# Attention heads taken in pairs, with projections cut into half units and a new merge order, in a two-layer hybrid trunk

## The chip, the cores and the metric

One Trainium2 chip, one core of it. The metric is the device time of the whole program in microseconds, median of the runs, lower is better. Two kernels of this case are told apart when they differ by over 0.2%.

## What is computed

Two layers, each of a half-step SwiGLU FFN, a token-mixing block and a second FFN, on x of 512 tokens by 1024 channels in float32. The mixing block reads one normalised input through one projection (`w_in`) and sums three gated branches:

```python
h = rms_norm(x, mix_norm[i])
z = h @ w_in[i]
y_a = dilated_attention_mixture(q, k, v)      # 3 groups x 4 heads of 64
y_b = spatial_gating(u, v, ...)               # chunked gMLP
y_c = multiscale_pool(z[..., C_OFF:G_OFF], ...)
gates = jax.nn.sigmoid(z[..., G_OFF:] + b_gate[i])
merged = (gates[0] * (y_a @ w_proj_a[i]) + gates[1] * (y_b @ w_proj_b[i])
          + gates[2] * (y_c @ w_proj_c[i]))
x = x + merged @ w_out[i]
```

In the attention, head slot j of the three groups is one softmax over all the keys of the three windows. The sequence is split into 4 residues r (tokens t with t mod 4 = r), so there are 4 x 4 = 16 (head, residue) items in a layer, `ATT = 16`, each with 128 queries and 768 keys (512 of group 0, 128 of each of the others).

## The kernel before, in words

**Large products.** A weight unit is 1024 x 256 float32, loaded to `raw[slot]` by SP's queue (`load`), then split in two parts: ScalarE (ACT) copies it rounded to `w_hi[slot]` (L737), VectorE (DVE) makes `w_lo = raw - w_hi` (L1030). TensorE (PE) does three products (hi*hi, lo*hi, hi*lo) for each of 2 column halves c and 8 k-tiles: 48 matmuls of 128x128 by 128x512 to a unit, into `psum[0]` or `psum[1]`. There are two slots, so a unit is split while the one ahead of it is multiplied: ACT's `split` waits for `unit_done` of the unit two back, PE's `unit()` waits for `split_made`, SP's `load` waits for `split_made` of the unit two back.

**The attention phase.** After the value projection and the three query/key units of heads 0 and 1, the remaining 6 units (3 query/key units of heads 2 and 3, 3 gate units of the first merge column) are interleaved with the 16 items. The order is written out by hand: 18 slots of 16 projection matmuls (L444, `part`), `attended(s)` says which item a slot holds. In a slot PE does: `scores` of the next item (L619: 3 float32 matmuls that read 64 rows of `qk`, 2 passes each, so 6 instructions, into `side[0]`), 8 projection matmuls, `transposes` of this item's probabilities (L629, 6 into `side[1]`), 8 projection matmuls, `values` (L641, 6 float32 matmuls in 12 instructions that write 64 rows of `side[1]`). DVE adds the mask and takes the maximum (L1340), negates it (L1344), later the reciprocal (L1349) and the scaling (L1350, `p_made`). ACT takes the exponential (L941), copies the transposed tile to `pT` (L963) and the head's output to `ya_hi` (L926); DVE makes `ya_lo` (L1329, `head_made`). Heads j even lie on rows 0 to 63 of `qk` and `side[1]`, j odd on rows 64 to 127. The order of items is head by head, four residues each, so that neighbours mostly share their rows. Projection outputs alternate between `psum[0]` and `psum[1]` by unit and DVE takes a whole unit (`take_unit`: L1309 twice, or L1052).

**The merge.** For each of 4 column pairs: gate units g = 0, 1, 2 from h (48 matmuls each), then `project`: `ya` (12 matmuls, w_proj_a), `yb` (24, w_proj_b), `yc` (24, w_proj_c). DVE multiplies the gates with them (L1392, L1395, L1401), ACT does the sigmoids (L934). Then 4 output units, banks in the order `OUT_BANKS`.

Of the kernel before, what the change touches and what calls it, by code (L numbers as in the profile page):

```python
# [18 lines left out]
F32 = mybir.dt.float32  # L19
# [56 lines left out]
def trunk(nc, x, ffn1_norm, ffn1_w_gate, ffn1_w_up, ffn1_w_down, mix_norm, w_in, b_gate, b_ln_g,  # L76
# [16 lines left out]
    ATT = HEADS * RES  # L93
    KEYS = S + 2 * P
# [5 lines left out]
    EV0, EV1 = 47, 47  # L100
# [4 lines left out]
    with ExitStack() as ctx:  # L105
# [48 lines left out]
        pT = at("pT", M + 42 * KB_, KEYS)  # L154
# [52 lines left out]
        unit_done = sem("unit_done")  # L207
        evacuated = [sem(f"evacuated{s}") for s in range(2)]
# [43 lines left out]
        SLOTS = 18  # L252
# [7 lines left out]
        OUT_BANKS = (2, 1, 0, 1)  # L260

        def attended(s):

            if s in (0, 9) or not 0 < s < SLOTS:
                return None
            return s - 1 if s < 9 else s - 2
# [6 lines left out]
        def _(sp):  # L273
# [40 lines left out]
            with rounds(sp, DEPTH, counts, split_made=UNITS_PER_LAYER) as layer:  # L314
# [83 lines left out]
        def _(pe):  # L398
# [39 lines left out]
            def part(dst, w, x_hi, x_lo, q0, q1):  # L438

                whi, wlo = w  # L440
                for q in range(q0, q1):
                    c, k, n = q // (3 * KD), q // 3 % KD, q % 3
                    l, r = ((whi, x_hi), (whi, x_lo), (wlo, x_hi))[n]
                    mm = nc.tensor.matmul(dst[:, c * S:(c + 1) * S], l[:, k * UNIT_N + c * P:k * UNIT_N + (c + 1) * P],  # L444
                                          r[:, k * S:(k + 1) * S], start=(k == 0 and n == 0), stop=(k == KD - 1 and n == 2))
                return mm

# [70 lines left out]
            with rounds(pe, DEPTH, counts, unit=UNITS_PER_LAYER, ev0=EV0, ev1=EV1,  # L518
                        sv0=8 + ATT, sv1=4, h=3 * D_PAIRS, acc=3 * (1 + KD), act=2 * FF_UNITS, w_sT=1, pooled=4,
                        vb=1, p=ATT, pT=ATT, head=ATT, y=2, merged=D_PAIRS) as layer:  # L520
# [88 lines left out]
                def scores(n):  # L609
                    j, r = divmod(n, RES)  # L610
                    rows_ = slice((j % 2) * HEAD_DIM, (j % 2 + 1) * HEAD_DIM)
                    t = qk[j // 2]
                    o = begin_side(0)
                    col = 0
                    for g in range(GROUPS):
                        q, k = g * S + r * P, (GROUPS + g) * S
                        keys = t[rows_, k:k + S] if g == 0 else t[rows_, k + r * P:k + (r + 1) * P]
                        width = S if g == 0 else P
                        mm = nc.tensor.matmul(o[:, col:col + width], t[rows_, q:q + P], keys, start=True, stop=True)  # L619
                        col += width  # L620
                    mm.then_inc(side_done[0], 1)

                def transposes(n):

                    pe.wait_ge(p_made, counts["p"].next())

                    pe.wait_ge(head_made, counts["head"].next())
                    for c in range(KEYS // P):
                        mm = nc.tensor.transpose(side[1][:, c * P:(c + 1) * P], p_tile[n % 2][:, c * P:(c + 1) * P], ident[:, :])  # L629
                    mm.then_inc(pT_written, 1)  # L630

                def values(n):
                    j, r = divmod(n, RES)

                    pe.wait_ge(pT_made, counts["pT"].next())
                    out_rows = slice((j % 2) * HEAD_DIM, (j % 2 + 1) * HEAD_DIM)
                    o = side[1][out_rows, KEYS:KEYS + P]
                    for c in range(KEYS // P):
                        g, t = (0, c) if c < TILES else (c - TILES + 1, r)
                        col = t * A_WIDTH + g * A_OUT + j * HEAD_DIM  # L640
                        mm = nc.tensor.matmul(o, v[:, col:col + HEAD_DIM], pT[:, c * P:(c + 1) * P],  # L641
                                              start=(c == 0), stop=(c == KEYS // P - 1))
                    mm.then_inc(head_done, 1)

                pair_of = (0, 1, 0, 1, 0, 1)
                STEP = 3 * 2 * KD // 6
                for s in range(SLOTS):
                    m, third = divmod(s, 3)
                    this, after = attended(s), attended(s + 1)
                    if third == 0:  # L650
                        o = begin(pair_of[m])
                        w = unit()
                    if this is not None and after is not None:
                        scores(after)

                    start, end = 2 * STEP * third, 2 * STEP * (third + 1)
                    before, between = (STEP, STEP) if s < SLOTS - 1 else (STEP // 2, STEP - 2)
                    part(o, w, h_hi, h_lo, start, start + before)
                    if this is None:
                        if s == 0:  # L660

                            pe.wait_ge(side_evacuated[1], counts["sv1"].now(1))

                        pe.wait_ge(evacuated[1 - pair_of[m]], counts[f"ev{1 - pair_of[m]}"].now(1))
                        scores(after)
                    else:
                        transposes(this)
                    mm = part(o, w, h_hi, h_lo, start + before, start + before + between)
                    if third == 2 and s < SLOTS - 1:
                        mm.then_inc(unit_done, 1)  # L670
                    if this is not None:
                        values(this)
                part(o, w, h_hi, h_lo, start + before + between, end).then_inc(unit_done, 1)

                def project():
# [3 lines left out]
                pe.wait_ge(head_made, counts["head"].now(1))  # L681
                pe.wait_ge(y_ready, counts["y"].next(2))
                project()
                with rounds(pe, D_PAIRS - 1, counts, unit=6, ev0=3, ev1=3):
                    for s in (1, 0, 1):
                        columns(begin(s), unit(), h_hi, h_lo, range(KD), True, True).then_inc(unit_done, 1)
                    project()
# [36 lines left out]
        def _(act):  # L724
# [105 lines left out]
            with rounds(act, DEPTH, counts, unit=UNITS_PER_LAYER, raw0=8 * UNITS_PER_LAYER + 16 * 2,  # L830
                        raw1=8 * UNITS_PER_LAYER + 16 * 3, ev0=EV0, ev1=EV1, se0=8 + ATT, act=2 * FF_UNITS,
                        sd0=7 + ATT, sd1=4, ln=1, yb=2, neg=ATT, pT_written=ATT, head=ATT, merged=D_PAIRS) as layer:
# [84 lines left out]
                counts["sd0"].next(ATT)  # L917
# [3 lines left out]
                def head_hi(n):  # L921
                    j, r = divmod(n, RES)
                    rows_ = slice((j % 2) * HEAD_DIM, (j % 2 + 1) * HEAD_DIM)
                    act.wait_ge(head_done, counts["head"].next())
                    dst = ya_hi[rows_, (j // 2) * S:(j // 2 + 1) * S].rearrange("p (i r) -> p r i", r=RES)[:, r, :]
                    nc.scalar.activation(dst, side[1][rows_, KEYS:KEYS + P],  # L926
                                         ACT.Copy).then_inc(ya_hi_made, 1)
# [10 lines left out]
                def exponential(n):  # L938

                    act.wait_ge(neg_max_made, counts["neg"].next())  # L940
                    nc.scalar.activation(p_tile[n % 2][:, :], p_tile[n % 2][:, :], ACT.Exp, bias=neg_max[:, n % 2:n % 2 + 1],  # L941
                                         accum_out=row_sum[:, n % 2:n % 2 + 1]).then_inc(exp_made, 1)

                bias_col = T_BGATE + layer * (3 * KD)
                next_unit = [dict(parts=2), dict(parts=2), {}, {}, {}, dict(k=KA)]
                for s in range(SLOTS):
                    m, third = divmod(s, 3)
                    if attended(s - 1) is not None:
                        head_hi(attended(s - 1))
                    if third == 0:  # L950
                        if m > 0:
                            counts["unit"].next()
                            if m - 1 < 3:
                                counts[f"ev{(m - 1) % 2}"].next()
                        split(**next_unit[m])
                    if third == 1 and m > 3:
                        sigmoids(m - 4, (m - 1) % 2, bias_col)
                    if third == 1 and m > 3:

                        exponential(attended(s + 1))  # L960
                    if attended(s) is not None:
                        act.wait_ge(pT_written, counts["pT_written"].next())
# [495 lines left out]
```

## Time and profile before

| | |
|---|---|
| median of 3 runs | 2417.64 us (2417.22 to 2418.68) |
| the profiled execution's own time | 2416.66 us |
| its span, first to last instruction | 2414.9 us |
| mean granted TensorE clock | 0.997 |
| busy: PE, PE's weight loads, DVE, ACT, POOL | 99%, 82%, 45%, 30%, 1% |
| chain that ended last | PE 97%, ACT 1%, DVE 1% |
| two attention phases | 129.66 us each, 288 of the large matmuls and 16 items in each |

The span is between the first and the last instruction of the profiled execution; what lies around it is 1.76 us. A matmul's record lasts longer than its turn on the engine, since matmuls are pipelined: what a matmul takes in a stream is the distance from its start to the next one's start. An item is a (head, residue) pair as above.

### The profile page before, as it was taken

How to read it: one execution, taken by the hardware profiler on the slowest of the kernel's cores; microseconds unless marked ns; L12 is line 12 of the kernel's file. 1: busy time of each engine (PE TensorE's matmuls, PEld its weight loads, DVE VectorE, ACT ScalarE, POOL GpSimd, SP SyncE). 2: the span in 40 equal slices, each digit the busy share in tenths (PEclk: the TensorE clock that was granted, in tenths of full speed). 3: DMA queues.
4: the chain of work that ended last, by engine and by line, in shares of the span. 5: the costliest groups of instructions: out<-in, count | busy, mean ns of one | idle time of the engine just before them, and what ended most of it. 6: DMA issues, size and time to landing. Idle time of an engine off the chain costs nothing.

```text
span 2414.9 us, 27466 instructions
## 1 busy us (share of the span) xinstructions
PE 2394.2 (99%) x11021; PEld 1969.6 (82%) x11021; DVE 1095.0 (45%) x1045; ACT 716.6 (30%) x665; POOL 30.5 (1%) x58
## 2 busy tenths in 40 slices
PE   7999999999999999999999999999999999999999
PEld 6888888887788888888888888888777888888887
DVE  7444435544454554443344443365544445544433
ACT  4222223323422332222232222232334223322222
POOL 4000000000000000000000000000000000000000
PEclk9999999999999999999999999999999999999999
DMA  4333223321132323322332332332312233232221
GB/s 141 94 97 104 81 98 122 95 81 40 40 104 87 114 89 102 104 89 95 96 101 91 104 100 84 96 116 79 88 31 66 83 109 109 91 104 91 96 96 65
DMA packets 229756, 221.81 MB, mean 92 GB/s; under 512 B 4161, under 2 KB 227505, under 8 KB 229681
## 3 DMA queue, kind: packets, MB, share of 16 engines
q1 hardware_dynamic: 225696, 215.29, 28.4%
q10 hardware_dynamic: 3984, 5.51, 0.7%
q8 instruction: 48, 0.79, 0.1%
q14 instruction: 28, 0.22, 0.0%
HBM read 218.69 MB, written 2.10 MB: 91 GB/s over the span
## 4 chain that ended last, share of the span: by engine, by line
PE 97%; ACT 1%; DVE 1%; issue 0%; DMA 0%; ACTq 0%; DVEq 0%
PE psum L433 83%; PE psum L444 5%; PE side L641 2%; PE psum L561 2%; PE side L619 2%; PE side L433 1%; PE psum L453 1%; PE side L629 1%; DVE acc L1087 0%; PE side L571 0%; PE side L543 0%; DMA x_in<-in_x_dram 0%; ACT gate L934 0%; PE side L582 0%; ACT L941 0%
## 5 line engine op out<-in xcount | busy, mean ns | idle before, releaser
L433 PE MATMUL psum<-h_hi,w_hi 128*128 128x512 f32 x1984 | 776.0, 391 | 8.7 <-DVE w_lo L1030 8.5
L433 PE MATMUL psum<-h_lo,w_hi 128*128 128x512 f32 x1984 | 772.8, 390 | 0.0
L433 PE MATMUL psum<-h_hi,w_lo 128*128 128x512 f32 x1984 | 772.7, 389 | 0.0
L1030 DVE TENSOR_TENSOR w_lo<-raw,w_hi 128x2048 fp32r<-128x2048 f32 (+2 forms) x224 | 470.9, 2102 | 338.5 <-ACT w_hi L737 337.8
L737 ACT ACTIVATE w_hi<-raw 128x2048 fp32r<-128x2048 f32 (+2 forms) x224 | 393.8, 1758 | 601.9 <-PE psum L433 578.1
L433 PEld LDWEIGHTS psum<-h_hi,w_hi 128*128 128x128 f32 x1984 | 373.0, 188 | 88.5 <-issue 9.2
L433 PEld LDWEIGHTS psum<-h_hi,w_lo 128*128 128x128 f32 x1984 | 373.0, 188 | 77.9
L433 PEld LDWEIGHTS psum<-h_lo,w_hi 128*128 128x128 f32 x1984 | 373.1, 188 | 77.7 <-issue 1.2
L433 PE MATMUL psum<-act_hi,w_hi 128*128 128x512 f32 x704 | 273.9, 389 | 0.0
L433 PE MATMUL psum<-act_lo,w_hi 128*128 128x512 f32 x704 | 273.9, 389 | 0.0
L433 PE MATMUL psum<-act_hi,w_lo 128*128 128x512 f32 x704 | 273.9, 389 | 0.0
L793 ACT ACTIVATE act_hi<-us 128x1024 f32 (+1 forms) x44 | 46.7, 1061 | 455.0 <-DVE us L1118 455.0
L1052 DVE TENSOR_TENSOR us<-psum,rstd 128x1024 f32<-128x1024 f32 x44 | 53.9, 1225 | 276.5 <-PE psum L433 276.5
L433 PEld LDWEIGHTS psum<-act_hi,w_lo 128*128 128x128 f32 x704 | 132.2, 188 | 27.5
L433 PEld LDWEIGHTS psum<-act_lo,w_hi 128*128 128x128 f32 x704 | 132.2, 188 | 27.5
L433 PEld LDWEIGHTS psum<-act_hi,w_hi 128*128 128x128 f32 x704 | 132.2, 188 | 27.2
L1052 DVE TENSOR_TENSOR gs<-psum,rstd 128x1024 f32<-128x1024 f32 x44 | 53.9, 1225 | 119.4 <-PE psum L433 118.9
L1120 DVE TENSOR_TENSOR act_lo<-us,act_hi 128x1024 f32 (+1 forms) x44 | 53.9, 1226 | 58.7 <-ACT act_hi L793 58.7
L755 ACT ACTIVATE us<-xT 128x1024 f32<-128x1024 f32 x24 | 25.4, 1059 | 185.1 <-DVE xT L1065 185.1
L444 PE MATMUL psum<-h_hi,w_hi 128*128 128x512 f32 x192 | 77.8, 405 | 0.0
L444 PE MATMUL psum<-h_hi,w_lo 128*128 128x512 f32 x192 | 77.7, 405 | 0.0
L444 PE MATMUL psum<-h_lo,w_hi 128*128 128x512 f32 x192 | 77.4, 403 | 0.0
(185 smaller groups left out, 1942.4 us busy)
## 6 DMA issues: line engine op xcount, KB each, us to landing
raw<-in_ffn_w_gate_dram SPq DMA_DIRECT2D x44, 1024.0 KB, 5.3
raw<-in_ffn_w_up_dram SPq DMA_DIRECT2D x44, 1024.0 KB, 5.3
raw<-in_w_in_dram SPq DMA_DIRECT2D x42, 1024.0 KB, 5.3
raw<-in_ffn_w_down_dram SPq DMA_DIRECT2D x32, 1024.0 KB, 4.9
raw<-in_ffn_w_down_dram SPq DMA_DIRECT2D x16, 768.0 KB, 4.2
raw<-in_w_in_dram SPq DMA_DIRECT2D x24, 512.0 KB, 4.4
raw<-in_w_out_dram SPq DMA_DIRECT2D x8, 1024.0 KB, 5.0
raw<-in_w_proj_b_dram SPq DMA_DIRECT2D x8, 512.0 KB, 3.4
```

Source lines behind the costliest of these rows:

```text
L433: mm = nc.tensor.matmul(dst[:, c * S:(c + 1) * S], l[:, a], r[:, b], start=first and k == ks[0] and n == 0, stop=last and k == ks[-1] and ...
L444: mm = nc.tensor.matmul(dst[:, c * S:(c + 1) * S], l[:, k * UNIT_N + c * P:k * UNIT_N + (c + 1) * P], r[:, k * S:(k + 1) * S], start=(k == ...
L453: mm = nc.tensor.matmul(o, l[:, k * P:(k + 1) * P], r[:, k * S:(k + 1) * S], start=(k == 0 and n == 0), stop=(k == KD - 1 and n == 2))
L561: mm = nc.tensor.matmul(d, l[:, k * S + t * P:k * S + (t + 1) * P], r[:, b], start=(k == 0 and m == 0), stop=(k == KD - 1 and m == 2))
L619: mm = nc.tensor.matmul(o[:, col:col + width], t[rows_, q:q + P], keys, start=True, stop=True)
L641: mm = nc.tensor.matmul(o, v[:, col:col + HEAD_DIM], pT[:, c * P:(c + 1) * P], start=(c == 0), stop=(c == KEYS // P - 1))
L737: nc.scalar.activation(w_hi[s][:, 0:k * n], raw[s][:, 0:k * n], ACT.Copy).then_inc(hi_made, 1)
L755: nc.scalar.activation(sq[:, :], pair(xT, d), ACT.Square).then_inc(sq_made, 1)
L793: nc.scalar.activation(pair(act_hi, i), us[:, :], ACT.Copy).then_inc(act_hi_made, 1)
L1030: nc.vector.tensor_tensor(w_lo[s][:, a], raw[s][:, a], w_hi[s][:, a].bitcast(F32), ALU.subtract).then_inc(split_made, 1)
L1052: return nc.vector.tensor_tensor(dst, two(psum[s][:, :]), rstd2, ALU.mult)
L1120: nc.vector.tensor_tensor(pair(act_lo, i), us[:, :], pair(act_hi, i).bitcast(F32), ALU.subtract).then_inc(act_ready, 1)
```

## The change

Items are taken as 8 pairs, `PAIRS = 8`: pair n holds residue r = n mod 4 of heads 2*jp and 2*jp+1, jp = n div 4. PE does both items' scores one after the other (the first into `side[0]`, the second into `psum[1]`), then both items' values of the pair ahead of it (`pT[0]`, `pT[1]`), then projection matmuls, then both items' transposes (into `side[1]`, then `side[0]`), then projection matmuls. All matmuls of the first head stand ahead of the second's. The 288 projection matmuls of the phase are one stream cut at positions `SCORES_AT` and `TURNS_AT`; their outputs go to the two halves of `psum[0]` alone, and DVE takes them by half unit (24 matmuls), told by `half_done` or `unit_done`. `ya_hi` and `ya_lo` are made once for a pair, on 128 rows. On ACT the copy of a pair's outputs (`head_hi`) and, for some pairs, the split of a unit stand ahead of the two exponentials. The merge order is yb, ya, yc with the banks swapped, and PE waits for the last head only ahead of the first ya. No arithmetic is added or taken away.

```diff
+    PAIRS = ATT // 2
-        pT = at("pT", M + 42 * KB_, KEYS)
+        pT = [at("pT0", M + 42 * KB_, KEYS), at("pT1", M + 85 * KB_, KEYS)]
+        half_done = sem("half_done")
+        scored_b = sem("scored_b")
-        SLOTS = 18
+        PHASE = 6 * 2 * 3 * KD
+        SCORES_AT = (10, 48, 86, 124, 162, 194, 226, 258)
+        TURNS_AT = (38, 76, 114, 152, 185, 217, 249, 281)
-        OUT_BANKS = (2, 1, 0, 1)
+        OUT_BANKS = (0, 2, 0, 1)
-                    for w in (w_proj_a, w_proj_b, w_proj_c):
+                    for w in (w_proj_b, w_proj_a, w_proj_c):
...
+                def project_to(end):
+                    for q in range(stream["at"], end):
+                        h, k, n = q // (3 * KD), q // 3 % KD, q % 3
+                        c = h % 2
+                        if q % (3 * KD) == 0:
+                            pe.wait_ge(evacuated[0], free + max(h - 1, 0))
+                            if c == 0:
+                                stream["w"] = unit()
...
+                        if k == KD - 1 and n == 2:
+                            mm.then_inc(half_done if c == 0 else unit_done, 1)
+                def score_pair(n):
+                    jp, r = divmod(n, RES)
+                    t = qk[jp]
+                    outs = (begin_side(0), begin(1))
+                    if n == RES:
+                        pe.wait_ge(evacuated[0], free + 6)
+                    for b in range(2):
+                        for g in range(GROUPS):
...
+                            mm = nc.tensor.matmul(outs[b][:, col:col + k1 - k0], t[rows_of(b), q:q + P], t[rows_of(b), k0:k1],
+                                                  start=True, stop=True)
+                            if g == GROUPS - 1:
+                                mm.then_inc((side_done[0], scored_b)[b], 1)
+                def turn_pair(n):
+                    pe.wait_ge(p_made, counts["p"].next())
...
+                    for c in range(KEYS // P):
+                        mm = nc.tensor.transpose(side[1][:, c * P:(c + 1) * P], p_tile[0][:, c * P:(c + 1) * P], ident[:, :])
+                    mm.then_inc(pT_written, 1)
+                    pe.wait_ge(p_made, counts["p"].next())
+                    o = begin_side(0)
...
+                def value_pair(n):
+                    pe.wait_ge(pT_made, counts["pT"].next())
+                    pe.wait_ge(side_evacuated[0], counts["sv0"].now(1 if n == PAIRS - 1 else 0))
                     pe.wait_ge(head_made, counts["head"].next())
+                    for b in range(2):
+                        for c in range(KEYS // P):
...
+                            mm = nc.tensor.matmul(side[1][rows_of(b), KEYS:KEYS + P], v[:, col:col + HEAD_DIM],
+                                                  pT[b][:, c * P:(c + 1) * P], start=(c == 0), stop=(c == KEYS // P - 1))
+                for n in range(PAIRS):
+                    project_to(SCORES_AT[n])
+                    score_pair(n)
+                    if n > 0:
+                        value_pair(n - 1)
+                    project_to(TURNS_AT[n])
+                    turn_pair(n)
+                project_to(PHASE)
+                value_pair(PAIRS - 1)
+                def project(last_head=False):
+                    columns(begin(1), unit(), yb_hi, yb_lo, range(KB), True, True).then_inc(unit_done, 1)
+                    if last_head:
+                        pe.wait_ge(head_made, counts["head"].now(1))
                     columns(begin(0), unit(), ya_hi, ya_lo, range(KA), True, True).then_inc(unit_done, 1)
-                    columns(begin(1), unit(), yb_hi, yb_lo, range(KB), True, True).then_inc(unit_done, 1)
-                    columns(begin(0), unit(), yc_hi, yc_lo, range(KB), True, True).then_inc(unit_done, 1)
+                    columns(begin(1), unit(), yc_hi, yc_lo, range(KB), True, True).then_inc(unit_done, 1)
...
+                for n in range(PAIRS):
+                    if n == 0:
+                        step(parts=2)
+                    if n > 0:
+                        head_hi(n - 1)
+                    if n == 1:
+                        step(parts=2)
+                    if n == 5:
+                        step()
+                    for b in range(2):
+                        exponential(b)
+                    if n in (2, 3):
+                        step()
+                    if n == 6:
+                        step(KB)
+                    take_turned()
+                    if n in (5, 6):
+                        counts["ev0"].next()
+                        sigmoids(n - 5, 0, bias_col)
+                head_hi(PAIRS - 1)
...
+                for n in range(PAIRS):
+                    score_max(n)
+                    if n > 0:
+                        head_lo(n - 1)
+                    normalise(0)
+                    normalise(1)
+                    if n < 4:
+                        take_half((0, 2, 3, 5)[n])
+                        split()
+                        if n in (0, 2):
+                            take_half((1, None, 4)[n])
+                    elif n in (4, 7):
+                        take_half(6 if n == 4 else 10)
+                        take_half(7 if n == 4 else 11)
+                    elif n == 5:
+                        split()
+                        take_half(8)
+                    else:
+                        take_half(9)
+                        split(KB)
+                head_lo(PAIRS - 1)
```

In this diff the second of the three blocks on ACT and the third on DVE (`for n in range(PAIRS)`) are each engine's own order. `take_turned` is ACT's copy of both transposed tiles (L963 twice), `score_max` DVE's masked maximum and negation for both items, `step` a split (ACT's L737).

## Rows read from the trace of the kernel before

**Rows 1.** The page: busy time of the engines, and the chain by engine.

```profile
PE 2394.2 (99%) x11021; PEld 1969.6 (82%) x11021; DVE 1095.0 (45%) x1045; ACT 716.6 (30%) x665; POOL 30.5 (1%) x58
PE 97%; ACT 1%; DVE 1%; issue 0%; DMA 0%; ACTq 0%; DVEq 0%
```

**Rows 2.** Both attention phases by windows: length, busy us (instructions), clock.

```profile
525.42:655.08 129.66, 128.27 (x674) 96.98 (x672) 57.04 (x127) 53.11 (x79) 0.00 (x0) 1.00 0.14 43
1715.17:1844.83 129.66, 128.26 (x673) 96.95 (x672) 57.04 (x127) 53.11 (x79) 0.00 (x0) 1.00 0.14 43
```

**Rows 3.** The chain in time order, first phase: start, length, what.

```profile
525.59 1.81 PE psum L444 x8
...
538.42 1.50 PE side L619 x6
539.92 2.04 PE psum L444 x8
541.96 0.66 PE side L629 x6
542.61 1.84 PE psum L444 x8
544.45 1.46 PE side L641 x12
```

**Rows 4.** Timeline of PE around group changes: start, length of the records.

```profile
544.06 0.39 PE L444 MATMUL psum<-h_hi,w_lo 128*128 128x512 f32 x1
544.38 0.32 PE L641 MATMUL side<-pT,v 128*64 128x128 f32 x1
...
545.63 0.27 PE L641 MATMUL side<-pT,v 128*64 128x128 f32 x1
545.84 0.69 PE L619 MATMUL side<-qk 64*128 64x512 f32 x1
546.37 0.81 PE L619 MATMUL side<-qk 64*128 64x512 f32 x3
...
547.13 0.27 PE L619 MATMUL side<-qk 64*128 64x128 f32 x1
547.33 0.50 PE L444 MATMUL psum<-h_hi,w_hi 128*128 128x512 f32 x1
547.67 0.40 PE L444 MATMUL psum<-h_lo,w_hi 128*128 128x512 f32 x1
```

**Rows 5.** Timeline of PE, three places where it waited for another engine.

```profile
592.36 0.69 PE L619 MATMUL side<-qk 64*128 64x512 f32 x1 [0.95 <-DVE qk L1309]
...
624.61 1.28 PEld L641 LDWEIGHTS side<-pT,v 128*64 128x64 f32 x12 [0.56 <-ACT pT L963]
...
647.45 0.19 PEld L641 LDWEIGHTS side<-pT,v 128*64 128x64 f32 x2 [0.73 <-ACT pT L963]
...
544.38 0.19 PEld L641 LDWEIGHTS side<-pT,v 128*64 128x64 f32 x2 [0.36 <-issue]
```

**Rows 6.** DVE and ACT by groups, 520 to 660 us: busy, mean ns.

```profile
L1340 DVE CUSTOM_DVE_ANT_0 p_tile<-side,masks 128x768 f32<-128x768 f32 x16 | 15.3, 954 | 9.6 <-issue 9.6
L1350 DVE TENSOR_SCALAR p_tile<-p_tile,small 128x768 f32<-128x768 f32 x16 | 9.9, 620 | 0.6
L941 ACT ACTIVATE p_tile<-p_tile,small 128x768 f32<-128x768 f32 x16 | 14.9, 931 | 4.7 <-DVE small L1344 4.7
L963 ACT ACTIVATE pT<-side 128x768 f32<-128x768 f32 x16 | 13.0, 811 | 43.8 <-PE side L629 43.8
L941 ACT ACT_TABLE_LOAD x3 | 3.8, 1283 | 0.1
```

**Rows 7.** Timeline of DVE and ACT, one split, one merge step.

```profile
546.13 1.92 ACT L737 ACTIVATE w_hi<-raw 128x2048 fp32r<-128x2048 f32 x1
...
655.28 1.23 DVE L1052 TENSOR_TENSOR gate<-psum,rstd 128x1024 f32<-128x1024 f32 x1 [0.78 <-PE psum L444]
656.42 1.22 DVE L1030 TENSOR_TENSOR w_lo<-raw,w_hi 128x1024 fp32r<-128x1024 f32 x1
```

More of the change, by code:

```diff
@@ L436, in columns @@
                 return mm
[L438 to L446, printed above, removed]
             def one_column(o, w):
@@ L623, in transposes @@
-                def transposes(n):
-                    pe.wait_ge(p_made, counts["p"].next())
-                    pe.wait_ge(head_made, counts["head"].next())
[L628 to L672, printed above, removed]
@@ L673, in _, with rows_of @@
-                part(o, w, h_hi, h_lo, start + before + between, end).then_inc(unit_done, 1)
-                def project():
+                def rows_of(b):
+                    return slice(b * HEAD_DIM, (b + 1) * HEAD_DIM)
+                free = counts["ev0"].next()
+                counts["ev0"].next(PHASE // (3 * KD) - 1)
+                stream = dict(at=0, w=None)
+                def project_to(end):
[6 more added lines that the diff above has]
+                                stream["w"] = unit()
+                        whi, wlo = stream["w"]
+                        l, r = ((whi, h_hi), (whi, h_lo), (wlo, h_hi))[n]
+                        mm = nc.tensor.matmul(psum[0][:, c * S:(c + 1) * S], l[:, k * UNIT_N + c * P:k * UNIT_N + (c + 1) * P],
+                                              r[:, k * S:(k + 1) * S], start=(k == 0 and n == 0), stop=(k == KD - 1 and n == 2))
+                        if k == KD - 1 and n == 2:
+                            mm.then_inc(half_done if c == 0 else unit_done, 1)
+                    stream["at"] = end
@@ L921, in head_hi @@
                 def head_hi(n):
[L922 to L927, printed above, removed]
+                    jp, r = divmod(n, RES)
+                    act.wait_ge(head_done, counts["head"].next(2))
+                    dst = ya_hi[:, jp * S:(jp + 1) * S].rearrange("p (i r) -> p r i", r=RES)[:, r, :]
+                    nc.scalar.activation(dst, side[1][:, KEYS:KEYS + P], ACT.Copy).then_inc(ya_hi_made, 1)
                 def sigmoids(g, s, col):
@@ L946, in _ @@
[L946 to L962, printed above, removed]
-                        nc.scalar.activation(pT[:, :], side[1][:, 0:KEYS], ACT.Copy).then_inc(pT_made, 1)
-                    if attended(s + 1) is not None and not (third == 1 and m > 3):
-                        exponential(attended(s + 1))
@@ L966, in _, with take_turned @@
-                head_hi(ATT - 1)
-                counts["unit"].next()
+                    nc.scalar.activation(p_tile[b][:, :], p_tile[b][:, :], ACT.Exp, bias=neg_max[:, b:b + 1],
+                                         accum_out=row_sum[:, b:b + 1]).then_inc(exp_made, 1)
+                def take_turned():
+                    act.wait_ge(pT_written, counts["pT_written"].next())
+                    nc.scalar.activation(pT[0][:, :], side[1][:, 0:KEYS], ACT.Copy).then_inc(pT_made, 1)
+                    act.wait_ge(pT_written, counts["pT_written"].next())
+                    nc.scalar.activation(pT[1][:, :], side[0][:, 0:KEYS], ACT.Copy).then_inc(side_evacuated[0], 1)
@@ L969, in project @@
+                head_hi(PAIRS - 1)
+                counts["ev0"].next()
                 def project(d, col):
-                    step(KB)
-                    sigmoids(2, 1, col)
+                    step(KA)
+                    sigmoids(2, 0, col)
                     step(KB)
                     step()
-                    counts["ev0"].next(2)
-                    counts["ev1"].next()
+                    counts["ev1"].next(2)
+                    counts["ev0"].next()
                     act.wait_ge(merged_made, counts["merged"].next())
@@ L984, in _ @@
                     for g in range(3):
-                        step(KA if g == 2 else UNIT_K)
+                        step(KB if g == 2 else UNIT_K)
                         if g < 2:
-                            sigmoids(g, 1 - g % 2, col)
+                            sigmoids(g, g % 2, col)
                     project(i + 1, col)
@@ L1010, in _ @@
                                            "silu", "act_hi", "gelu", "ln_std", "yc_hi", "yb_hi", "exp",
-                                           "head", "gate", "merged", "pooled", "y")}
+                                           "head", "gate", "merged", "pooled", "y", "half", "scored_b")}
             counts |= {k: Count(1) for k in ("ev0", "ev1", "se0", "se1")}
@@ L1348, in normalise @@
+                    dve.wait_ge(evacuated[1], v_)
+                    negate(1)
+                def normalise(b):
                     dve.wait_ge(exp_made, counts["exp"].next())
-                    chain(nc.vector.reciprocal(row_inv[:, b], row_sum[:, b]))
-                    nc.vector.tensor_scalar(p_tile[n % 2][:, :], p_tile[n % 2][:, :], row_inv[:, b], None,
+                    chain(nc.vector.reciprocal(row_inv[:, b:b + 1], row_sum[:, b:b + 1]))
+                    nc.vector.tensor_scalar(p_tile[b][:, :], p_tile[b][:, :], row_inv[:, b:b + 1], None,
@@ L1368, in _ @@
-                for s in range(SLOTS):
-                    m, third = divmod(s, 3)
-                    if attended(s - 1) is not None:
-                        head_lo(attended(s - 1))
-                    if third == 0 and m > 0 and attended(s) is None:
-                        take_unit(m - 1)
-                    if attended(s + 1) is not None:
-                        score_max(attended(s + 1))
-                    if third == 0:
-                        split(UNIT_K if m < 5 else KA)
-                        if m > 0 and attended(s) is not None:
-                            take_unit(m - 1)
-                    if attended(s + 1) is not None:
-                        normalise(attended(s + 1))
@@ L1387, in project @@
+                head_lo(PAIRS - 1)
                 def project(d):
+                    step(KA)
+                    dve.wait_ge(gate_made, counts["gate"].next(2))
+                    evac(1, nc.vector.tensor_tensor(gate[1][:, :], gate[1][:, :], psum[1][:, :], ALU.mult))
                     step(KB)
-                    dve.wait_ge(gate_made, counts["gate"].next())
-                    evac(0, nc.vector.tensor_tensor(gate[0][:, :], gate[0][:, :], psum[0][:, :], ALU.mult))
-                    step(KB)
```

117 lines of the change are left out of this document (58 added, 59 removed).

## The prediction, made blind

> **What bounds the kernel now.** I read the page first: PE is busy 99% of the span and is 97% of the chain that ended last, while DVE and ACT are at 45% and 30% [rows 1]. The reader is to see that time can only come out of PE's own stream. Then the windows on the two attention phases: 129.66 us each, clock 1.00 (that is 2.4 GHz), PE never truly idle [rows 2]. Busy shares can't say more, so I went to the chain in order of time and to the timeline of PE, where starts can be subtracted.
>
> The large matmuls follow each other at 1.81 / 8 = 0.227 us [rows 3]. One ordinary item takes 1.50 + 2.04 + 0.66 + 1.84 + 1.46 = 7.50 us [rows 3]. What would its instructions take if they merely followed each other? 16 large matmuls: 3.63. Scores: two passes of 512 columns and four of 128. Records two to four of them begin 0.54 apart, the last three 0.11 apart, so 2 x 0.43 + 4 x 0.11 = 1.30 [rows 4]. Transposes 0.65, near their row. Values 12 x 0.109 = 1.31 (544.38 to 545.63 is 1.25 for 11 steps, the first being longer) [rows 4]. Sum 6.89. So 0.61 us of each item is paid for changing between kinds of matmul. The starts show where [rows 4]: large matmul to values 0.32 in place of 0.23 (0.09) and a long first step (0.05); values to scores 0.21 in place of 0.11 (0.10); first to second score 0.53 in place of 0.43 (0.10); scores to large 0.20 in place of 0.11 (0.09); first to second large 0.34 in place of 0.23 (0.11). That is 0.54, and some 0.06 is spread over the large matmuls behind a change. The transposes cost nothing of the kind: they use the whole array, as the large ones do.
>
> For the phase: 288 x 0.2267 + 16 x 3.26 = 65.3 + 52.1 = 117.4, so 129.66 - 117.4 = 12.2 us are overhead. Of these about 1.5 are true waits: 0.95 for DVE's `qk` ahead of the scores of the ninth item, and two waits for ACT's `pT` beyond the ordinary 0.36: 0.56 - 0.36 = 0.20 and 0.73 - 0.36 = 0.37 [rows 5]. The other 10.7 are the changes, 0.67 an item.
>
> **Fewer changes of kind.** In a pair, large -> scores A, B -> values A, B -> large -> transposes A, B -> large: the chain of changes that one item paid is paid once for two. Eight pairs pay 8 x 0.54 = 4.3 us. The spread part of 0.06 an item I keep at 1.0. Overhead after: 5.3 in place of 10.7, a gain of 5.4 us a layer.
>
> **The waits that go.** The ninth item's scores no longer stand right behind the last query/key unit: half 5 ends at position 144, DVE takes it in pair 3, and pair 4's scores stand at 162, 18 matmuls or 4 us on. The two `pT` waits came of sigmoids and two table loads (1.28 us each [rows 6]) ahead of the copy on ACT; now the sigmoids stand behind the copy. Gain 1.5 us a layer, if no wait takes their place (next part).
>
> **The switch of head inside a pair** has no row: no two neighbours in the trace use different 64-row halves for scores or different output halves for values. There are 2 such switches in each of 16 pairs. Below: the second head's first instruction starts together with the first head's last, and saves one 0.11 step: 32 x 0.11 = -3.5 us. Above: each costs what a change of kind costs around scores (0.10 + 0.10): 32 x 0.20 = +6.4 us. The nearest row is the passage between large matmuls and transposes, same kind of use of the array and no cost; I take 0.
>
> The Trainium skill, TensorEngine Tiling (Array Packing), Key Properties, says that changing the tiling mode drains the engine and that changing only the tile does not, and that different tiles run in parallel. The 0.2 us steps of rows 4 agree with the first half. By its second half the sum would go to the low bound, 3.5 us lower; by the row of same-kind passages it is 0.
>
> **Does a new wait arise?** From a pair's first score S, by the rows: A's scores end at S + 1.6, B's at S + 2.9; DVE's maxima (0.95 and small steps) end at 2.8 and 4.1. Values of the pair before run from 2.8 to 5.6. ACT is held behind them: `head_hi` 5.7 to 6.1, then exponentials (0.93 and 0.1 for the sum) to 7.1 and 8.1 [rows 6]. DVE scales (reciprocal, then 0.62) by 8.0 and 9.0. PE reaches the transposes after 28 large matmuls, at 5.66 + 28 x 0.227 = 12.0 (23 in pairs 4 to 7: 10.9), B's at 11.6. Slack 1.9 us or more. Pairs 1 and 5 have a split (1.92 [rows 7]) ahead of the exponentials: scaled at 9.9 and 10.9 against 10.9 and 11.6 in pair 5, slack 0.6. Pair 6 has a table load, 1.28: slack 1.2. Behind the transposes ACT copies both tiles (2 x 0.81): the second ends 1.2 us after them, the next scores come 9 or 10 matmuls later, 2.1 us, and the last values 7 matmuls later, 1.7 us, slack 0.45. ACT's split in pair 3 waits for the unit that ends at position 144, 10.6, and ends at 12.5, when PE is only at the first transpose. DVE: in pairs 0 and 2 it waits in `take_half` until a half unit is over, some 15.1 at the latest, and ends at 16.1; the next pair's first maximum is due at 15.7 + 1.6 = 17.3 (pair 0: 14.2 against 14.5). The halves' banks are free one pair ahead. DMAs: every load still waits on the split two units back, 10 us or more before its own split. Price of all that: 0; if the cover in pair 5 were gone, 1 us for each 1 us of lateness, twice.
>
> **The half-size work.** `head_hi` and `head_lo` do 128 rows in one instruction, 16 fewer of each; neither is on the path: 0. Half-unit takes cost DVE the same operations, gates in two halves a little more, against 57 us of work in 129.66 [rows 2]: 0.
>
> **The merge order.** Before, `yb` (w_lo 1.22 us) is split while `ya`'s 12 matmuls (2.72 us) run, behind a take of 1.14: 656.42 + 1.22 = 657.64 against yb's start at 655.08 + 2.75 [rows 7]. After, it is `yc` that is split under `ya`, behind the product with gate 1, same lengths: slack again 0.15. Nothing gained or lost. At entry yb (5.4 us) covers the last head's copies, where six large matmuls did: 0 in both. If the slack failed: 0.2 us at 8 places, 1.6 us.
>
> **Sum.** 2 x (5.4 + 1.5) = 13.8 us. Against the profiled execution: span 2414.9 - 13.8 = 2401.1, with 1.76 around it 2402.9. The median shown stands 0.98 above that execution, so 2403.8.
>
> **The rivals.** (a) *Tiles overlap at the switch of head*: 2403.8 - 3.5 = 2400.3. For it the separate array halves, against it no row. Chance 0.25. (b) *The switch of head costs like a change of kind*: 2403.8 + 6.4 = 2410.2. For it that every other change among float32 groups cost 0.2; against it the free passage to the transposes. Chance 0.10. (c) *The gain is eaten by waits in some pairs*: pair 5 or 6 late by 1 to 2 us in both layers, some 2407. Chance 0.07. (d) *Slower*: PE stands at each pair's first transpose, because the path scores, maximum, values of the pair before, copy, exponential, scaling now holds two heads and ACT's `head_hi` stands ahead of both exponentials. It decides from 0.9 us a pair (13.8 / 16), which needs the path 1.9 + 0.9 = 2.8 us longer than its rows: 2420 if it is 3.2. Only the split's pairs come near. Chance 0.03. (e) *The phase is bound otherwise than by changes*, so that pairing moves nothing but the 3 us of waits: 2414.6; the starts in rows 4 speak against it. Chance 0.02. The forecast itself: 0.53.
>
> **Numbers.** The range goes from 2399.5 (a, with 0.8 for the sum's rounding) to 2408.5, leaving out most of (b), (d), (e) and a tail: 0.84 inside. The measurement tells 0.2%, 4.8 us; faster by more than that is all but (d), (e) and a little of (c): 0.94; within 0.03; slower 0.03.
>
> **What the profile after would show.** Attention phases of 122.7 us in place of 129.66; a pair of 15.7 us (14.4 in pairs 4 to 7); one 0.2 us step each at scores -> values and values -> large, none inside a pair (rival a: the second head's first record starts within some ns of the first's last; rival b: 0.2 to 0.3 apart). Waits of PE on `p_tile` or `pT` above 0.5 us would be (c) or (d). The merges should keep their lengths. The prediction is wrong if the phase is above 125 or below 120 us, or if time moves anywhere else.

## The result and the profile after

The changed kernel takes 2394.68 us (median of 4 runs, 2393.36 to 2395.02) against 2418.16 us for the kernel before in the same comparison: ratio 0.9902, 95% interval 0.9885 to 0.9919. It is 23.5 us faster. The forecast was 2403.8 us with a range down to 2399.5; the direction was right, the gain was 1.7 times the one forecast. Times of one kernel vary: its runs lie up to 1.7 us apart here, so the small effects below rest on lengths in the traces.

The first attention phase by windows, in the kernel after (columns as in [rows 2]); the second, 1703.99 to 1821.18, is as long:

```profile
525.86:643.05 117.19, 117.19 (x673) 92.94 (x671) 56.80 (x122) 48.87 (x70) 0.00 (x0) 1.00 0.16 48
```

Each phase has gone from 129.66 to 117.19 us, 12.47 us less, at the same clock. My sum said 122.7, and named a phase below 120 as a sign of being wrong. The phase even ended under the 117.4 us that I had worked out for a stream without any overhead, so instructions must run beside each other. The chain in order of time shows where, in one whole pair:

```profile
553.75 2.32 PE psum L616 x10
556.07 1.16 PE side L634 x3
557.23 0.11 PE psum L634
557.34 0.22 PE side L634 x2
557.57 0.97 PE psum L634 x5
558.54 2.38 PE side L663 x24
560.92 6.62 PE psum L616 x28
567.54 0.65 PE side L645 x6
568.19 0.66 PE side L650 x6
```

L616 are the large matmuls, L634 the scores (the first head's into `side`, the second's into `psum`), L663 the values, L645 and L650 the transposes. Read the four score lines: three of the first head's six instructions, then one of the second's, and only then the rest of the first's. A pair's scores take 1.16 + 0.11 + 0.22 + 0.97 = 2.46 us, where the terms of my sum come to 2.80 (1.50 for the first head, 1.30 for the second); 24 value instructions take 2.38, where they come to 2.77 (1.46 and 1.31). The timeline has the same seam by starts:

```profile
556.00 0.69 PE L634 MATMUL side<-qk 64*128 64x512 f32 x1
...
556.97 0.69 PE L634 MATMUL psum<-qk 64*128 64x512 f32 x1
557.07 0.49 PE L634 MATMUL side<-qk 64*128 64x128 f32 x3
```

The second head's first score (556.97) starts 0.1 us ahead of the last three of the first head, though it stands behind them in the program.

No wait took the place of the old ones: in the list of waits of this phase PE waits for no other engine, nor in that of the second phase, which answers to [rows 5]. The path over DVE and ACT was as worked out: in the tightest pair, pair 5, the scaled probabilities are ready 8.8 and 9.7 us after the first score, and PE comes for them at 10.2 and 10.9.

One thing got worse. In the merges, `yc` now starts late (DVE's timeline, then PE's weight loads, kernel after; these answer to [rows 7]):

```profile
695.32 1.22 DVE L1414 TENSOR_TENSOR gate<-gate,psum 128x1024 f32<-128x1024 f32 x1 [3.78 <-PE psum L432]
696.46 1.22 DVE L1037 TENSOR_TENSOR w_lo<-raw,w_hi 128x1024 fp32r<-128x1024 f32 x1
```

```profile
697.23 0.19 PEld L432 LDWEIGHTS psum<-ya_hi,w_lo 128*128 128x128 f32 x1
697.73 0.19 PEld L432 LDWEIGHTS psum<-yc_hi,w_hi 128*128 128x128 f32 x1 [0.32 <-DVE w_lo L1037]
```

`ya` starts at 694.96; DVE's product starts 0.36 us later, not 0.20 as a take did behind `ya` before, so `w_lo` is finished at 697.68, when PE already wants it. Together with a slower restart of PE that is some 0.2 us at three of the four merges of a layer, and 0.1 at the first, where the product starts 0.29 us behind `ya`. From the first `ya` or `yb` to the output units, layer 1 takes 153.18 us in place of 152.45, layer 2 153.13 in place of 152.43. Together 1.4 us lost.

The two traced executions differ by 21.6 us in span (2414.9 and 2393.3), less than the 24.9 us of the two phases minus 1.4. Of the 1.9 us between, 0.4 lie ahead of the first phase and 1.3 behind the last merges. There, in both kernels, the granted clock fell from 1.00 to 0.50 (1.2 GHz) while PE did its last transposes, 6.5 us ahead of the end in the kernel before and 9.9 us ahead of it in the kernel after, and the transposes then follow each other at 0.21 us in place of 0.11.

### The profile page after: what moved, and what is told of

It reads as the page before. It is cut to its first block, busy times and chain, and to the rows that moved or that the text cites. A ratio compares the mean times of both kernels' runs of the same rounds, so it can differ in the third digit from the quotient of the medians.

```text
span 2393.3 us, 27568 instructions
## 1 busy us (share of the span) xinstructions
PE 2374.8 (99%) x11021; PEld 1962.3 (82%) x11021; DVE 1091.7 (46%) x1035; ACT 707.8 (30%) x649; POOL 28.5 (1%) x58
## 4 chain that ended last, share of the span: by engine, by line
PE 98%; DVE 1%; DMA 0%; ACT 0%; issue 0%; ACTq 0%; DVEq 0%
PE psum L432 83%; PE psum L616 6%; PE psum L550 2%; PE side L663 2%; PE side L634 1%; PE side L432 1%; PE psum L442 1%; PE psum L634 1%; PE side L650 0%; PE side L645 0%; DMA x_in<-in_x_dram 0%; DVE acc L1094 0%; PE side L560 0%; PE side L532 0%; PE side L571 0%; DVE h_lo L1085 0%
## 5 line engine op out<-in xcount | busy, mean ns | idle before, releaser
L616 PE MATMUL psum<-h_hi,w_lo 128*128 128x512 f32 x192 | 76.4, 398 | 0.0
L616 PE MATMUL psum<-h_lo,w_hi 128*128 128x512 f32 x192 | 76.3, 397 | 0.0
L616 PE MATMUL psum<-h_hi,w_hi 128*128 128x512 f32 x192 | 76.2, 397 | 0.0
```

The lines of the kernel that those rows point to most:

```text
L616: mm = nc.tensor.matmul(psum[0][:, c * S:(c + 1) * S], l[:, k * UNIT_N + c * P:k * UNIT_N + (c + 1) * P], r[:, k * S:(k + 1) * S], start=( ...
```

## The experiments

All compare with the kernel before on the same chip (its medians there: 2417.34, 2416.95 and 2417.06 us in the three groups of four) and are told by their own median and phase length. The groups ran on different chips and the medians of the kernel before differ by up to 1.2 us between them and the first comparison, so a difference of that size between two groups tells nothing. "Theory" numbers start from 2394.7, the changed kernel's time. The edits are on the changed kernel, but for the one that says otherwise.

### Taking the overlap away at the scores

```diff
-  mm = nc.tensor.matmul(outs[b][:, col:col + k1 - k0], t[rows_of(b), q:q + P], t[rows_of(b), k0:k1],
+  mm = nc.tensor.matmul(outs[b][:, col:col + k1 - k0], t[rows_of(0), q:q + P], t[rows_of(0), k0:k1],
```

> Edit: in each pair the second head's score matmuls read the first head's 64 rows of qk (so both heads' scores are those of the first head), nothing else changes. Theory 1 (the 5.6 us a layer beyond my sum come from the second head's instructions running beside the last ones of the first, because they use other rows of the array): the overlap at the scores goes, the block of a pair's scores is 2.79 us as my sum had it in place of the 2.46 seen, phase 117.2 + 8 x 0.33 = 119.8 us, time 2394.7 + 5.3 = 2400. Theory 2 (the changes between kinds of matmul are cheaper in the new order, no overlap): nothing changes, 2394.7.

Measured: 2399.31 us, ratio 0.9924 (0.991 to 0.9937), phase 119.62 us. The chain of that kernel:

```profile
556.78 1.50 PE side L634 x6
558.28 1.30 PE psum L634 x6
559.58 2.38 PE side L663 x24
```

The first head's six now stand whole ahead of the second's six, 2.80 us together, as my sum had them. The values are untouched. What this kernel has and the changed one has not is one and the same set of rows for both heads, so the 2.4 us a phase are overlap of two row halves. The two heads still write different tiles (`side` and `psum`) in it, so those alone don't make the overlap.

### Taking it away at the values

```diff
-  mm = nc.tensor.matmul(side[1][rows_of(b), KEYS:KEYS + P], v[:, col:col + HEAD_DIM],
+  mm = nc.tensor.matmul(side[1][rows_of(0), KEYS:KEYS + P], v[:, col:col + HEAD_DIM],
```

> Edit: in each pair the second head's value matmuls write the first head's 64 output rows of the bank, so the second head's result takes the first's place and the other 64 rows keep what an earlier use left. Theory 1 (overlap of different array halves): the block of a pair's values is 2.76 us in place of 2.39, phase 117.2 + 8 x 0.37 = 120.2 us, time 2394.7 + 6 = 2400.7. Theory 2 (cheaper changes of kind): 2394.7.

Measured: 2399.11 us, 0.9926 (0.9912 to 0.9939), phase 120.03 us; the 24 value instructions take 2.76 us again:

```profile
558.78 2.76 PE side L663 x24
```

In this kernel the second head also writes the very addresses that the first wrote, so this run alone can't tell the shared half from the shared addresses. No run separates the two; at the scores the addresses stayed apart and the overlap went all the same.

### Both away: my own sum, measured

Both edits at once.

> Edit: both earlier edits together: the second head's scores read the first head's rows of qk and its values write the first head's output half (its result takes the first's place). All of the change stands but no two matmuls can use different halves of the array. Theory 1 (my sum for fewer changes of kind and vanished waits is right, 13.8 us, and the rest is overlap): phases of 119.6 + 120.0 - 117.2 = 122.4 us (my sum said 122.7), time 2394.7 + 10.5 = 2405. Theory 2 (the changes of kind are worth more than my sum and the two overlaps share a part): below 2401.

Measured: 2405.01 us, 0.9951 (0.9937 to 0.9964), phase 122.57 us, the sum having said 122.7. This is the kernel I had forecast: pairs, fewer changes of kind, no waits, no overlap. The chain, one pair:

```profile
557.07 1.50 PE side L634 x6
558.57 1.30 PE psum L634 x6
559.87 2.76 PE side L663 x24
```

The two single edits add (2.43 + 2.84 = 5.27 us of phase, 5.38 measured together). Two heads one after the other on the same half have no step between them, which is the 0 that my sum took; what it missed is what different halves give.

### One more change of kind

Four large matmuls moved between a pair's scores and the values of the pair before.

```diff
                     if n > 0:
+                        project_to(SCORES_AT[n] + 4)
                         value_pair(n - 1)
```

> Edit: four of the large projection matmuls move from behind a pair's values to between its scores and the values of the pair before (7 of 8 pairs); same matmuls, one more passage scores -> large -> values in place of scores -> values. Theory 1 (each change of kind costs what my starts gave: 0.09 and 0.11 and 0.09 more, 0.09 less, and 0.02 to 0.05 over the next ones): 0.22 x 7 x 2 = 3.1 us more, 2397.8, and up to 0.6 more if the later values make pair 5 wait. Theory 2 (changes of kind cost nothing, all of the gain was overlap and waits): 2394.7.

Measured: 2396.82 us, 0.9917 (0.9903 to 0.993), phase 118.63 us: 1.44 us more for 7 places, 0.21 us each (expected 0.22), 2.9 us in two layers. The time alone is 2.1 us more, which the noise between groups would not settle; the phase does. So one passage more has the price that the starts of [rows 4] gave it.

### The new merge order on the kernel before

```diff
-                    for w in (w_proj_a, w_proj_b, w_proj_c):
+                    for w in (w_proj_b, w_proj_a, w_proj_c):
...
-                    columns(begin(0), unit(), ya_hi, ya_lo, range(KA), True, True).then_inc(unit_done, 1)
-                    columns(begin(1), unit(), yb_hi, yb_lo, range(KB), True, True).then_inc(unit_done, 1)
+                    columns(begin(0), unit(), yb_hi, yb_lo, range(KB), True, True).then_inc(unit_done, 1)
+                    if last_head:
+                        pe.wait_ge(head_made, counts["head"].now(1))
+                    columns(begin(1), unit(), ya_hi, ya_lo, range(KA), True, True).then_inc(unit_done, 1)
...
-                    dve.wait_ge(gate_made, counts["gate"].next())
-                    evac(0, nc.vector.tensor_tensor(gate[0][:, :], gate[0][:, :], psum[0][:, :], ALU.mult))
+                    dve.wait_ge(gate_made, counts["gate"].next(2))
+                    evac(0, nc.vector.tensor_tensor(gate[1][:, :], gate[1][:, :], psum[0][:, :], ALU.mult))
```

> Edit: the kernel before with the new merge order alone (yb, ya, yc; loads, splits, gates and the wait for the last head moved with it). Theory 1 (the merge order is worth nothing): 2417.3. Theory 2 (ya first cost something at entry or in the splits): 1 to 2 us faster, 2416.

Measured: 2419.34 us over 11 runs against 2416.95, ratio 1.0009 (1.0000 to 1.0018): not faster, rather 2.4 us slower, at the edge of what the interval tells. Neither theory had this sign. The trace has the same late start as the changed kernel:

```profile
711.70 0.19 PEld L433 LDWEIGHTS psum<-yc_hi,w_hi 128*128 128x128 f32 x1 [0.32 <-DVE w_lo L1031]
```

The merges of the two layers are 0.65 and 0.59 us longer than in the kernel before, 1.2 us together. In this execution the first phase was also 1.58 us longer than the second, and that is the clock: from 594.9 to 598.3 us the granted clock was 0.50 (1.2 GHz), which happened inside a phase in no other trace of this case, and large matmuls follow each other there at 0.43 us in place of 0.23. PE had just waited 0.96 us for DVE's `qk`, but it waited as long in the kernel before, where the clock stayed at 1.00. So the 1.58 us are no part of the edit, and the other 1.2 us of the median's 2.4 stay open.

### The gate wait put ahead

```diff
-                    step(KA)
-
-                    dve.wait_ge(gate_made, counts["gate"].next(2))
+                    split(KA)
+                    dve.wait_ge(gate_made, counts["gate"].next(2))
+                    done()
```

> Edit: the changed kernel with DVE's wait for the two sigmoids ahead of its wait for yb's matmuls in the merge, so that one wait and not two lies between the end of yb and the product with gate 1. Theory 1 (in the new merge order that product starts 0.36 us after yb's successor ya and not 0.20 as before, so yc's w_lo is finished 0.05 us too late and PE's restart makes it 0.2 us a merge): 8 x 0.18 = 1.4 us less, merges of 5.44 us for yc, time 2393.3. Theory 2 (the slow start of yc has another cause): yc stays at 5.57, 2394.7.

Measured: 2393.02 us, 0.9898 (0.9883 to 0.9913). `yc` takes 5.44 to 5.49 us at every merge (before this edit 5.53 to 5.62). The same two operations, and PE's first load of `yc`:

```profile
695.18 1.22 DVE L1414 TENSOR_TENSOR gate<-gate,psum 128x1024 f32<-128x1024 f32 x1 [3.62 <-PE psum L432]
696.32 1.22 DVE L1037 TENSOR_TENSOR w_lo<-raw,w_hi 128x1024 fp32r<-128x1024 f32 x1
```

```profile
697.59 0.19 PEld L432 LDWEIGHTS psum<-yc_hi,w_hi 128*128 128x128 f32 x1 [0.15 <-DVE w_lo L1037]
```

`ya` starts at 694.98 here: the product now comes 0.20 us behind it and `yc`'s first load 0.14 us earlier than in the changed kernel. The wait for the sigmoids had nothing to wait for: ACT ended the last of them 2.5 us before `ya` started, in both kernels. The cause is shown by its places, and the merges of the two layers are 0.63 and 0.65 us shorter, 1.3 us together (expected 1.4); that the time is 1.7 us less agrees, but the two intervals overlap.

### Heads alternating, scores

```diff
-                    for b in range(2):
-                        for g in range(GROUPS):
+                    for g in range(GROUPS):
+                        for b in range(2):
```

> Edit: a pair's score matmuls alternate between the two heads (A1 B1 A2 B2 A3 B3) in place of A1 A2 A3 B1 B2 B3. Theory 1 (whatever stands within a few instructions and uses other rows runs beside it): two heads' scores take about one head's time, 1.30 + 0.1 + 0.2 = 1.6 us in place of 2.46 for a pair, 16 pairs, 2394.7 - 13.8 = 2381. Theory 2 (only the seam gains and every alternation costs as a change does, 0.1 to 0.2 us, 4 more of them in a pair): 2394.7 + 16 x 0.6 = 2404. Theory 3 (it makes no difference how they are ordered): 2394.7.

Measured: 2379.13 us, 0.984 (0.9826 to 0.9853), phase 109.50 us. Theory 1, with a little more than it promised (15.5 us in place of 13.8).

### Heads alternating, values

```diff
-                    for b in range(2):
-                        for c in range(KEYS // P):
+                    for c in range(KEYS // P):
+                        for b in range(2):
```

> Edit: a pair's value matmuls alternate between the two heads, 128 keys of each at a time. Theory 1 (overlap of different output halves): 1.31 + 0.05 + 0.2 = 1.56 us in place of 2.39 for a pair, 16 pairs: 2394.7 - 13.3 = 2381.4. Theory 2 (each alternation costs 0.1 or more, 10 more of them): 2394.7 + 16 = 2411. Theory 3 (only the depth of the overlap seen at the seam counts, no more): 2394.7.

Measured: 2379.23 us, 0.984 (0.9827 to 0.9854), phase 109.44 us; the 24 instructions take 1.46 us, those of a single item took 1.46 for 12 [rows 3].

### How far ahead PE looks: blocks of three and of two

```diff
-                    for b in range(2):
-                        for c in range(KEYS // P):
+                    for b, c in [(b, c) for c0 in range(0, KEYS // P, 3) for b in range(2) for c in range(c0, c0 + 3)]:
```

> Edit: the changed kernel with a pair's values in blocks of three matmuls (six instructions) of each head in turn, scores as changed. Theory 1 (an instruction can start once the one four places ahead of it has started, if the array half it needs is free: that is what the seam shows, where B's first starts with A's fourth from the last): two steps of 0.109 more than full alternation, 1.46 + 0.22 = 1.68 us a pair, 2379.2 + 3.5 = 2382.7. Theory 2 (each seam gains the 0.37 us seen, there are three now): 2.76 - 1.11 = 1.65, 2382.2, but with the first head's first block alone for four steps, not two.

Measured: 2384.5 us, 0.9862 (0.9847 to 0.9878), 1.73 us for the 24 (expected 1.68). The first record of the second head is at 558.247 beside the first head's third at 558.241, as theory 1 placed it; theory 2 had it two steps later. The block is 0.05 us longer than the two steps of theory 1, and the time 1.8 us above its 2382.7: by the phase, 111.96 us, a pair costs 0.32 us more than when alternating, where theory 1 had 0.22. So the rule gives the place, and not all of the price.

With 2 for 3 in the same line:

> Edit: the same in blocks of two matmuls (four instructions) of each head. Theory 1 (look ahead of four places): the second head's first instruction starts with the first head's first, as in full alternation: 1.46 us a pair, 2379.2. Theory 2 (0.37 us a seam, nothing to do with places; five seams, 1.85 us, but not below one head's time): also near 2379, so it is the start of the second head's first record, beside the first's first or not, that tells. Theory 3 (the look ahead is three places, not four): one step of 0.109 more in each block, 16 x 0.33 = 5 us more, 2384.

Measured: 2379.89 us, 0.9843 (0.983 to 0.9856), 1.51 us for the 24. The second head's first starts at 557.574, the first head's first at 557.560, so they start together: the fifth instruction starts with the first, and theory 3 (three places) is out. That it is no more than four places was told by the longer blocks: with five, the second head would have started beside the second instruction in blocks of six.

### Both alternating, then with the gate wait

> Edit: scores and values of a pair both alternate between the heads. Theory 1 (the two savings add): phases of 109.5 + 109.4 - 117.2 = 101.8 us, time 2394.7 - 30.9 = 2363.8. Theory 2 (a pair is now 1.9 us shorter, but the path of maximum, copy, exponential and scaling is not, so PE waits for p_tile in the pairs that have a split or a table load ahead of the exponentials, 0.5 to 1 us in each of up to 3 pairs a layer): 2365 to 2370.

Measured: 2363.02 us, 0.9777 (0.9763 to 0.979), phase 101.64 us (expected 101.8). No wait arose. Score starts of one pair, first head and second (their next instructions start at 553.62 and 553.63):

```profile
553.09 0.69 PE L634 MATMUL side<-qk 64*128 64x512 f32 x1
553.10 0.69 PE L634 MATMUL psum<-qk 64*128 64x512 f32 x1
```

> Edit: scores and values of a pair alternate between the heads, and DVE's wait for the sigmoids stands ahead of its wait for yb. Theory 1 (the two edits have nothing in common and add): 2363.0 - 1.4 = 2361.6, 0.977 of the kernel before. Theory 2 (a shorter phase leaves the first merge late, where the last pair's copies and splits come close): no gain from the second edit, 2363.0.

Measured: 2361.64 us, 0.9768 (0.9755 to 0.9781), `yc` at 5.44 to 5.46 us: 55 us faster than the kernel before, 33 us faster than the changed one, and the best version here.

## Why the prediction was wrong, point by point

**What bounds the kernel: right.** The two phases are 24.9 us shorter, and all of that is PE's stream.

**Fewer changes of kind, and waits gone: right in mechanism and size.** 5.4 + 1.5 = 6.9 us a layer were forecast. With the overlap taken away the phase is 122.57 us, 7.1 us less than 129.66: 14.2 us against 13.8. The price of one passage was measured again at 0.21 us by adding seven a layer. One part of the 5.4 had no row: the starts of [rows 4] give 8 x 0.54 = 4.3, the other 1.1 is what remained of the 10.7 us, and the 122.57 us say that it went too.

**The switch of head inside a pair: the step that failed.** I took 0 for it in the sum and, as the low bound, one step of 0.11 us for each of 32 switches, 3.5 us. A switch saves 0.30 us at the scores (119.62 - 117.19 over 8 pairs) and 0.36 at the values (120.03 - 117.19 over 8), 10.8 us in all when both are taken away together. Two things were wrong in my term. I let the nearest row, large matmuls followed by transposes, stand for a case it does not resemble: both of those use 128 rows and 128 columns, so that row says nothing of two different halves. And in the rival I let the second head start only together with the first head's last instruction, while it starts beside the fourth from last. The rule of the Trainium skill, TensorEngine Tiling (Array Packing), Key Properties, that different tiles load and multiply in parallel, is what the trace shows, with 24 value instructions in 1.46 us where one half alone needs 2.76. I had given it as a sentence beside the rival and a chance of 0.25; the runs say that it should have carried the forecast. Even so the rival's size was too small: its 2400.3 us is 5.6 us above the time measured.

**The bound that was too near.** A bound for something no row shows has to ask for the most that the mechanism could do, not for its smallest instance. Two heads beside each other all the way give 42 us against no overlap (2405.01 us with both heads on one half, 2363.02 with the heads alternating on two). The changed kernel keeps the heads in blocks and gets 10.8 of them; the forecast's range had no room for any of it beyond one step of 0.11 us a switch.

**No new wait: right.** The slack of the tightest pair was forecast at 1.0 and 0.7 us (10.9 against 9.9, 11.6 against 10.9, for which the prediction wrote 0.6), it is 1.4 and 1.2. That is not the overlap's doing, which moves both ends: in the kernel without overlap the probabilities are scaled at 9.5 and 10.5 and taken at 10.9 and 11.6, a slack of 1.4 and 1.1. My path was 0.4 us too long. In rival (d) one number is wrong: a path longer by 3.2 us gives 16 x 1.3 = 20.8 us and 2424.6 us, not 2420.

**The merge order: mis-sized.** I gave it 0 and a slack of 0.15 us, with 1.6 us as the price if the slack failed. It failed: DVE passes two waits between the end of `yb` and its product, and starts 0.36 us after `ya` in place of 0.20; by the rows the slack was 0.19 (657.83 against 657.64), and 0.16 of it went there. The price was near the one stated, 1.4 us.

Together: 14.2 us from pairing and the vanished waits, 10.8 us from overlap, 1.4 us lost in the merges, 23.6 against 23.5 measured. That they agree to 0.1 us is partly luck, since the runs of one kernel lie 1 to 2 us apart.

## What to carry to other kernels

Where two small matmuls use different halves of the array (other 64 rows for the operands, or other 64 output rows), let them alternate in the program: here the second one was nearly free (31.7 us on top of the change, 33 with the merge repair). Different output halves were tried only within one tile, `side`, and different operand rows only with outputs in two tiles. Blocks of one head at a time get only the few instructions at the seam. Grouping matmuls by kind is worth 0.2 us for each passage saved; and a wait that is already satisfied is not free (0.16 us here) when it stands in a path with a tenth of a microsecond of slack, so put it ahead of the one that is waited for.

## What the runs showed of the hardware that was not expected

Matmuls do not always start in program order. The second head's first score started at 556.97 us, ahead of three score instructions of the first head that stand before it (557.07 and on). It goes ahead by a fixed number of places: an instruction on a free half starts once the one four places before it has started (values in blocks of twelve: beside the ninth, 559.395 and 559.389 us; scores and values in blocks of six: beside the third; values in blocks of four: beside the first). Why it is four, no run shows. Alternating, the starts of the two halves are 0.01 us apart and both run at their full rate, for float32 scores of 512 columns as for values of 128.

One more passage between kinds of matmul costs PE 0.21 us even if no engine waits.

A wait on DVE that had been satisfied 2.5 us earlier still delayed the operation behind it by 0.16 us (0.09 at the first merge of a layer), when it stood behind the wait that ended last.
